# Two layers written out, norms of two groups of 280 tokens beside half tiles, and latent attention in 16 steps

## What is computed

```python
h = rmsnorm(x, g_pre_mix)
qn, qr, ckv, kr, qb, kb, vb, qc, kc, vc, alr, gc, gate = split(h @ w_in)
oa = latent_attention(qn, qr, ckv, kr)          # 8 heads, chunks of 64, meta tokens, rope
ob = windowed_attention(qb, kb, vb, sinks)      # 8 query heads, 2 key heads
loga = log_sigmoid(alr @ w_alpha + b_alpha) / 16
oc = rmsnorm(gla_scan(qc, kc, vc, loga, s0), g_gla) * silu(gc)   # 4 heads, state 128 x 256
g = sigmoid(gate)
y = g[0] * (oa @ w_up_a) + g[1] * (ob @ w_up_b) + g[2] * (oc @ w_up_c)
x = x + rmsnorm(y @ w_out, g_post_mix)
f = square(relu(rmsnorm(x, g_pre_mlp) @ w_ff1)) @ w_ff2
x = x + rmsnorm(f, g_post_mlp)
```

## Time and profile before

| | |
|---|---|
| median of 3 runs | 2607.6 us |
| the profiled execution, its own time | 2612.26 us |
| its span | 2610.5 us |
| TensorE busy | 2465.8 us |
| TensorE's mean granted clock | 0.971 |
| VectorE, ScalarE, GpSimd busy | 984.5, 943.5, 1123.3 us |
| weight splits on GpSimd | 298 of 2402 ns |

### The profile page before, as it was taken

The page is one execution under the profiler, slowest core; times in us unless marked ns, Lnnn a source line. Parts: engine busy times, 40 slices in busy tenths (PEclk is TensorE's granted clock), DMA queues, the critical chain, the costliest instruction groups (busy, mean ns, idle before and its releaser), DMA issues.

```text
span 2610.5 us, 42794 instructions
## 1 busy us (share of the span) xinstructions
PE 2465.8 (94%) x17996; PEld 2280.5 (87%) x17996; DVE 984.5 (38%) x1746; ACT 943.5 (36%) x1757; POOL 1123.3 (43%) x677
## 2 busy tenths in 40 slices
PE   7999999999999799999879999999999997999997
PEld 6999878798798799999779998878977997999996
DVE  4566435435622411111355555444256124111113
ACT  4344423332444432322334443333333544322322
POOL 5433223333355464544343432233334455645543
PEclk8999999999999899999989999999999998999998
DMA  4111311121123122222121114111211231222222
GB/s 149 56 63 55 105 54 49 45 69 56 41 73 116 42 88 89 82 89 82 64 81 57 62 56 118 41 49 47 75 49 41 81 108 49 82 89 86 85 90 84
DMA packets 57464, 189.45 MB, mean 73 GB/s; under 512 B 8048, under 2 KB 12880, under 8 KB 56624
## 3 DMA queue, kind: packets, MB, share of 16 engines
q1 hardware_dynamic: 47120, 165.90, 19.5%
q10 hardware_dynamic: 10144, 20.73, 2.5%
HBM read 172.44 MB, written 10.89 MB: 70 GB/s over the span
## 4 chain that ended last, share of the span: by engine, by line
PE 44%; DVE 3%; POOL 2%; ACT 1%; issue 1%; DVEq 0%; POOLq 0%
PE dense L695 35%; PE att L743 1%; PE att L930 1%; PE att L991 1%; DVE h_raw L1530 1%; PE att L881 1%; PE att L820 1%; POOL h_lo L1860 1%; PE att L806 0%; POOL wlo L1855 0%; DVE x L1513 0%; PE att L947 0%; PE att L964 0%; PE att L824 0%; PE att L997 0%
## 5 line engine op out<-in xcount | busy, mean ns | idle before, releaser
L1855 POOL TENSOR_TENSOR wlo<-wraw,whi 128x1024 fp32r<-128x1024 f32 x298 | 715.4, 2402 | 947.5 <-ACT whi L1060 947.5
L695 PE MATMUL dense<-h_hi,whi 128*128 128x280 f32 x3200 | 947.4, 296 | 17.5 <-ACT cproj L1098 8.3
L695 PE MATMUL dense<-h_lo,whi 128*128 128x280 f32 x3200 | 938.8, 293 | 0.0
L695 PE MATMUL dense<-h_hi,wlo 128*128 128x280 f32 x3200 | 936.6, 293 | 0.0
L695 PEld LDWEIGHTS dense<-h_hi,whi 128*128 128x128 f32 x3200 | 607.5, 190 | 41.3 <-issue 16.4
L695 PEld LDWEIGHTS dense<-h_hi,wlo 128*128 128x128 f32 x3200 | 606.4, 189 | 1.5 <-issue 0.8
L695 PEld LDWEIGHTS dense<-h_lo,whi 128*128 128x128 f32 x3200 | 607.0, 190 | 0.0
L1060 ACT ACTIVATE whi<-wraw 128x1024 fp32r<-128x1024 f32 x298 | 312.5, 1049 | 294.6 <-DMA wraw<-in_w 256.0
L695 PE MATMUL dense<-hid_lo,whi 128*128 128x280 f32 x1024 | 298.4, 291 | 0.0
L695 PE MATMUL dense<-hid_hi,whi 128*128 128x280 f32 x1024 | 297.8, 291 | 0.0
L695 PE MATMUL dense<-hid_hi,wlo 128*128 128x280 f32 x1024 | 297.6, 291 | 0.0
(11 more groups left out here) (290 smaller groups left out, 3619.5 us busy)
## 6 DMA issues: line engine op xcount, KB each, us to landing
wraw<-in_w SPq DMA_DIRECT2D x305, 512.0 KB, 3.4
x_spill<-x ACTq DMA_DIRECT2D x2, 2240.0 KB, 7.9
x<-x_spill ACTq DMA_DIRECT2D x2, 2240.0 KB, 9.2
k_cat<-k_rope ACTq DMA_DIRECT2D x16, 212.0 KB, 3.5
x<-in_x SPq DMA_DIRECT2D x4, 560.0 KB, 5.4
out_y_out<-x SPq DMA_DIRECT2D x1, 2240.0 KB, 7.3
out_c_out<-ckv ACTq DMA_DIRECT2D x2, 560.0 KB, 6.6
const<-in_const SPq DMA_DIRECT2D x1, 1112.0 KB, 10.9
```

The source lines that it names most:

```text
L695: mm = pe.matmul(bank[0:m, 0:HALF], a[:, k, o * 128:o * 128 + m], b[:, k, H[hf]], start=(k == 0 and i == 0), stop=(k == kt - 1 and i == 2))
L1855: pool.tensor_tensor(wlo[slot][:, :], wraw[slot][:, :], whi[slot][:, :].bitcast(F32), ALU.subtract).then_inc(pool_done, st.done("pool", f" ...
```

## The change

The two layers are written out in one program: the plan is one list over both layers and the work ahead of them, with its own name space for each layer (`st.layer`). The device loop, its barrier and the cleared semaphores are gone. All parameters of both layers are loaded at the start.

The five last units of `out`, the five first of `ff1`, the five last of `ff2` and the five first of a layer run as half-tiles (`("half", u, hf)`). While the second halves of the five units of `out` run, tokens 0 to 279 get the norm and are split; while the first halves of `ff1` run, tokens 280 to 559 do. The same is done from `ff2` to the next layer, where the first half of the five units of the new layer stands ahead of unit 0's second half and of `p z`. The sums of squares of the new x are made on VectorE in a buffer `nsum` and then take one matmul per half (`mean_square`), where TensorE did the sum before. `h_lo` of slices 2 and 5 is VectorE's, the other six are GpSimd's. The six PSUM banks of `SIX` serve as dense banks for `out`, `ff1`, `ff2` and the first five units of a layer, and weights have up to ten more buffers in these stretches (`slots_for`). In the prologue the same halves are used, and x comes in four quarters.

In the first head, `p z` stands behind the second half of unit 0, and four half-tiles stand between it and `p lev 0`, which also waits for the evacuations of these units. GpSimd's three memsets stand in `v arg 0`, behind VectorE's scan. The parts of head 0 behind `p vtok` (`p kv`, `p o`, `p ms`) stand one unit later than before.

The latent attention has 16 jobs; that of the first frame tile holds the 48-query tile of its pair too, and every step has its dense unit. `y` is split behind each unit of `up_b`, to `oc_hi` and `oc_lo`. The last layer has no `mean`; its x is stored by four DMAs, two for each half of the tokens.

```diff
-wraw = [at(f"wraw{s}", [P, 1024], F32, r_w[s]) for s in range(WSLOTS)]
-wlo = [at(f"wlo{s}", [P, 1024], F32R, r_w[s]) for s in range(WSLOTS)]
-whi = [at(f"whi{s}", [P, 1024], F32R, r_w[s] + 4096) for s in range(WSLOTS)]
+BASE, MLP, MIX, EDGE = range(0, 3), range(3, 5), range(5, 9), range(9, 13)
+w_at = r_w + [work + 24 * row + 8192 * i for i in range(2)] + [work + 8192 * i for i in range(4)] + [r_oc + 8192 * i for i in range(4)]
+wraw = [at(f"wraw{s}", [P, 1024], F32, w_at[s]) for s in range(len(w_at))]
...
+    def y_engine_of_lo(k):
+        return "dve" if k >= 6 else "pool"
+    def token_lo_engine(k):
+        return "dve" if k in (2, 5) else "pool"
...
+    plan = []
+    U_MIX, V_MLP = [UIDX["out", n] for n in range(KD - LAP, KD)], [UIDX["ff1", n] for n in range(LAP)]
+    U_MLP, V_NEXT = [UIDX["ff2", 32 - LAP + n] for n in range(LAP)], list(range(LAP))
+    JOBS = {"a": [("a", t, i) for t in range(4) for i in range(4)], "b": [("b", kv, i) for kv in range(2) for i in range(5)]}
+    jobs = JOBS["a"]
+    def lap(l, post, pre, first, second):
+        for hf, (at_l, units) in enumerate((first, second)):
+            for i, u in enumerate(units):
+                plan.append((at_l, ("half", u, 1 - hf)))
+                if i == 0:
+                    plan.extend([(l, ("ms", post, hf)), (l, ("norm", post, hf))])
+                if i == LAP - 2:
+                    plan.extend([(l, ("ms", pre, hf)), (l, ("tokens", pre, hf))])
...
+        order.append(("half", 0, 1))
+        gla_steps((0, "p z"), (0, "v decay"), (0, "v arg 0"))
+        for u in V_NEXT[1:]:
+            order.append(("half", u, 1))
+            if UNITS[u][0] == "cq":
+                gla_steps((0, "v arg 1"))
+            if UNITS[u][0] == "ck":
+                gla_steps((0, "v lev 0"), (0, "v arg 2"), (0, "v lev 1"), (0, "v end"), (0, "v lev 2"))
+        gla_steps((0, "p lev 0"), (0, "v kend"), (0, "v amat 0"), (0, "v amat 1"), (0, "v amat 2"))
...
+        for j in range(len(JOBS["a"]) + 2):
+            order.append(("att", "a", j))
+            dense()
...
+        for u in range(next(dn), NU):
+            kind, n = UNITS[u]
+            if u in V_MLP:
+                continue
+            plan.append((l, ("half" if u in U_MIX + U_MLP else "dense", u) + ((0,) if u in U_MIX + U_MLP else ())))
+            if kind == "up_b":
+                plan.append((l, ("split_y", n)))
+            if u == U_MIX[-1]:
+                lap(l, "post_mix", "pre_mlp", (l, U_MIX), (l, V_MLP))
+                plan.extend([(l, ("half", v, 1)) for v in V_MLP])
+        if l + 1 < DEPTH:
+            lap(l, "post_mlp", "next", (l, U_MLP), (l + 1, V_NEXT))
+            plan.append((l, ("spill",)))
+        else:
+            for i, u in enumerate(U_MLP):
+                plan.append((l, ("half", u, 1)))
+                if i == 0:
+                    plan.extend([(l, ("ms", "post_mlp", 0)), (l, ("norm", "post_mlp", 0))])
+            plan.extend([(l, ("ms", "post_mlp", 1)), (l, ("norm", "post_mlp", 1))])
+    plan += [(-1, ("square", 0)), (0, ("w", 0)), (-1, ("ms", "next", 0)), (-1, ("tokens", "next", 0)), (0, ("w", 1)),
+             (-1, ("square", 1)), (0, ("half", 0, 0)), (0, ("w", 2)), (-1, ("ms", "next", 1)), (-1, ("tokens", "next", 1)),
+             (0, ("half", 1, 0)), (-1, ("spill",)), (0, ("w", 3)), (0, ("half", 2, 0)), (0, ("w", 4)), (0, ("half", 3, 0)), (-1, ("masks",)), (0, ("half", 4, 0))]
+    for l_ in range(DEPTH):
+        layer_plan(l_)
...
+    def slots_for(l, u):
+        kind, n = UNITS[u]
+        if kind in ("out", "ff1", "ff2"):
+            if kind == "out" or (kind == "ff1" and n < 8):
+                return [*MLP, *MIX] if u in U_MIX else [*BASE, *MIX] if u in V_MLP else [*BASE] if kind == "out" else [*BASE, *MLP]
+            if kind == "ff2" and n >= 24:
+                return [*MLP, *EDGE] if u in U_MLP else [*BASE]
+            return [*BASE, *MLP]
+        return [*BASE, *EDGE] if u in V_NEXT else [*BASE]
...
+        wide = kind in ("out", "ff1", "ff2") or u in V_NEXT
+        b = min(SIX if wide else TWO, key=lambda c: bank_free[c])
...
+    def tiles_of(br, i):
+        return (0, 4) if br == "a" and i == 0 else (i,)
...
+        ys = io["y_out"].rearrange("(k p) t -> p k t", p=P)
+        for hf in range(2):
+            for g in range(2):
+                for e, k in (("dve", 4 * g + 2), ("pool", 4 * g + 3)):
+                    sp.wait_ge(by_name[e], A(e, f"x post_mlp {k} {hf}", DEPTH - 1))
+                sp.dma_start(ys[:, 4 * g:4 * g + 4, H[hf]], x[:, 4 * g:4 * g + 4, H[hf]]).then_inc(last_stored, 16)
+        sp.wait_ge(last_stored, 64)
...
-        def norm(which):
-            for hf in range(2):
-                pe.wait_ge(dve_done, A("dve", f"sum {which} 7 {hf}"))
-                mm = pe.matmul(ps[:, S0 + hf, 0:HALF], c_("ones_d"), sqsum[:, H[hf]], start=True, stop=True)
-            mm.then_inc(pe_done, st.done("pe", f"ms {which}"))
-        def mean(which):
-            for k in range(KD):
-                pe.wait_ge(act_done, A("act", f"sq {which} {k}"))
-                for hf in range(2):
-                    mm = pe.matmul(ps[:, T0 + hf, 0:HALF], c_("ones_d"), sq[:, k, H[hf]],
-                                   start=(k == 0), stop=(k == KD - 1))
-            mm.then_inc(pe_done, st.done("pe", f"ms {which}"))
+        def mean_square(which, hf):
+            part = 0 if which.startswith("post") else 1
+            pe.wait_ge(dve_done, A("dve", f"sum {which} 7 {hf}"))
+            if l < 0 and hf == 0:
+                pe.wait_ge(ones_loaded, 32)
+            mm = pe.matmul(ps[:, S0 + hf, 0:HALF], c_("ones_d"), nsum[:, part, H[hf]], start=True, stop=True)
+            mm.then_inc(pe_done, st.done("pe", f"ms {which} {hf}"))
...
+                if h == 0:
+                    for u in V_NEXT:
+                        e = evac_engine(UNITS[u][0])
+                        pe.wait_ge(by_name[e], A(e, f"evac {u} 0 1"))
...
+                    if i == 0:
+                        mm = pe.matmul(ps[0:MIXED, S0 + a, 144:144 + K_META], q_cat[:, h, META0:T], k_cat[:, h, 0:K_META],
+                                       start=False, stop=True, skip_group_check=True)
...
+        def add_square_x(which, k, hf):
+            dve.wait_ge(act_done, A("act", f"sq {which} {k} {hf}"))
+            if k >= 2:
+                dve.wait_ge(dve_done, A("dve", f"sum {which} {k - 1} {hf}"))
+            if k >= 1:
+                total = nsum[:, 1, H[hf]]
+                dve.tensor_tensor(total, total, nsum[:, 3, H[k % 2]], ALU.add).then_inc(dve_done, st.done("dve", f"sum {which} {k} {hf}"))
+        def norm(which, hf):
             src = norm_src[which]
-            dve.wait_ge(act_done, A("act", f"rstd {which}"))
+            pre = None if which == "post_mlp" and l + 1 == DEPTH else "pre_mlp" if which == "post_mix" else "next"
+            dve.wait_ge(act_done, A("act", f"rstd {which} {hf}"))
             if which == "post_mix":
-                dve.wait_ge(x_back, 16)
-                for hf in range(2):
-                    dve.wait_ge(act_done, A("act", f"evac {UIDX['out', 7]} 0 {hf}"))
+                dve.wait_ge(x_back, 16 * (l + 1))
+                dve.wait_ge(act_done, A("act", f"evac {UIDX['out', KD - 1]} 0 {hf}"))
+            else:
+                dve.wait_ge(dve_done, A("dve", f"evac {UIDX['ff2', 31]} 0 {hf}"))
             for k in range(KD):
-                t = src[:, k, :]
-                dve.scalar_tensor_tensor(t, t, p_("g_" + which, k), rstd[:, :], ALU.mult, ALU.mult
-                                         ).then_inc(dve_done, st.done("dve", f"nrm {which} {k}"))
+                t = src[:, k, H[hf]]
+                dve.scalar_tensor_tensor(t, t, p_("g_" + which, k), rstd[:, H[hf]], ALU.mult, ALU.mult
+                                         ).then_inc(dve_done, st.done("dve", f"nrm {which} {k} {hf}"))
                 if x_engine(k) == "dve":
-                    dve.wait_ge(dve_done, A("dve", f"nrm {which} {k}"))
-                    dve.tensor_tensor(x[:, k, :], x[:, k, :], t, ALU.add).then_inc(dve_done, st.done("dve", f"x {which} {k}"))
+                    dve.wait_ge(dve_done, A("dve", f"nrm {which} {k} {hf}"))
+                    dve.tensor_tensor(x[:, k, H[hf]], x[:, k, H[hf]], t, ALU.add).then_inc(dve_done, st.done("dve", f"x {which} {k} {hf}"))
+                if pre and k >= 3:
+                    add_square_x(pre, k - 2, hf)
+            if pre:
+                add_square_x(pre, KD - 2, hf)
+                add_square_x(pre, KD - 1, hf)
...
-            if s == "v decay" and h == 0:
+            if s == "v arg 0" and h == 0:
+                pool.wait_ge(dve_done, A("dve", "gla scan 0"))
...
-with nc.Fori(0, DEPTH) as l:
-    with nc.Block() as block:
-        layer(l, block)
-    for s_ in block_sems:
-        nc.sync.sem_clear(s_)
-    nc.all_engine_barrier()
...
+    program(block)
```

917 lines of the change are left out of this document (481 added, 436 removed).

## The result

| | before | after |
|---|---|---|
| median | 2607.31 us (2604.98 to 2607.72, 4 runs) | 2562.81 us (2561.44 to 2563.57, 4 runs) |
| ratio to before | | 0.9831, 95% interval 0.9814 to 0.9848 |
| span of the profiled execution | 2610.5 us | 2561.7 us |

The change saves 44.5 us of the forecast 73.7. The time lies inside the range (2490 to 2575) and outside the forecast's own (2515 to 2555), next to the rival of serial engines (2565). The parts of the sum say more than the total. The profiled executions differ by 48.8 us, of which these parts make 46.6.

The account below looks back on a forecast made before the run. TensorE, busy 2465.8 of 2610.5 us, was taken as the bound, with 215.6 us of stage losses. Savings 16.7 + 12.6 + 27 + 18.4 + 10, less 5 and 6, make 73.7: 2612.3 - 73.7 - 4.7 = 2534 us, range 2490 to 2575.

Parts of the forecast that it names:

- rival of serial engines: Half crossings: VectorE and GpSimd run one after the other, each half losing 15 us; 43 saved, 2565 us; chance 0.13.
- The steady rate: Dense matmuls in all stages: 128.3 ns each, 6.16 us per weight tile of 48, unchanged by the change.
- the attention: Latent attention in 16 steps, each with a dense tile covering TensorE's wait: saves 27 us, bounds 10 to 32.
- y: From y to out: splitting y behind each up_b tile leaves a loss of 1 us; saves 12.6, bounds 8 to 13.6.
- the tail: Behind the last tile: less work and half the tokens normed earlier leave 15.2 us; saves 16.7, bounds 12 to 20.
- the first head's wait: Before head 0's level products: a 25.0 us chain beside 12.3 us of half-tiles leaves TensorE idle 12.7 us.
- rest of the GLA heads: Next head: mean square directly ahead of its level products, with rstd between, costs 2.5 us a layer, 5 in all.
- h = 9.7: Average loss in us of one half crossing, of six; taken from (2 x 20.3 + 17.7) / 6.
- a sign of being wrong: Crossing halves losing under 5 us or over 15 would show the forecast wrong.
- 6.6: First half of a crossing: about 26 us elapsed for 19.7 us of TensorE work, so 6.6 us lost.
- 13.7: Second half of out to ff1: weight split and three linked ReLU evacuations ahead of rstd, 13.7 us lost.
- The prologue: Start to the first level products: first dense matmul some 9 us earlier, yet costs 6; bounds 14 lost to 10 gained.

Follow-up runs that it names:

- att_gap: The changed kernel with three latent-attention steps per layer (5, 9, 13) left without their dense tile, which runs behind the attention: 2580.73 us, ratio 0.9878.
- norm_first: The changed kernel with the branch norm of the second half of out to ff1 issued ahead of the first ff1 half-tile's evacuation: 2561.23 us, ratio 0.9802.
- tokens_first: The changed kernel with out to ff1's whole second-half chain (rstd, norm, rstd, splits) ahead of the ff1 half-tiles' evacuations and weight splits there: 2545.25 us, ratio 0.9728.
- lev_late: The changed kernel with one more whole tile ahead of the first head's level products in both layers: 2533.83 us, ratio 0.9691.

## Why the prediction was right in part

**Right.** The steady rate; the attention, y and the tail within 1 us each; the first head's wait (12.4 and 10.8 us, forecast 12.7) and its mechanism, a chain that the tiles beside it don't cover; the direction of every part. For the attention only half of the gain is shown to come from the mechanism that was forecast (att_gap).

**Right by luck.** The rest of the GLA heads cost 5.3 us for a forecast 5 (2.5 a layer), but layer 0 lost 8.1 and layer 1 gained 2.8. The forecast mechanism, a wait for rstd of 1.52 us ahead of the next head's level products, is there in both layers. In layer 0 a stretch at a lower granted clock followed it and in layer 1 none, 17.06 against 12.23 us for the same instructions:

```profile
138.58:155.64 17.06, 17.06 (x105) 16.99 (x105) 9.80 (x16) 1.06 (x1) 4.82 (x2) 0.70 0.08 27
1409.03:1421.26 12.23, 12.23 (x104) 12.16 (x105) 11.86 (x16) 1.06 (x1) 4.37 (x2) 1.00 0.10 35
```

In norm_first, the same program up to 840 us, that stretch of layer 0 takes 12.25 us. So 4.8 of the 5.3 come and go between executions.

**The half crossings.** The step that failed is h = 9.7. By the windows above it is 12.7 (76.3 us for six), 18 us too little. Two of the six, 17.8 and 15.5, are over the 15 that the prediction itself named as a sign of being wrong. Its terms for the norm and splits were good: VectorE's norm with its sums ran from 850.91 to 861.2, 10.3 us (10 taken), the splits from 863.40 to 871.66, 8.3 us (7). The whole first half of layer 0, from the end of the last half-tile to the end of the first that uses the half, took 26.2 us for a forecast of about 26. That it lost 7.7 and not 6.6 is a slip of counting: the prediction took off 19.7 us of TensorE's work where the six half-tiles, taken off here and in the loss before the change, are 18.5. If it did so in all six halves (its text shows it for the one), 7 of the 18 us are this slip. What was mis-sized besides stands around the norm and splits:
- In the second half of out to ff1 rstd stands twice behind linked evacuations. I counted three of 1.3 us and one split of 2.40; the first rstd came 4.2 us after its matmul and the second 6.5, since every evacuation waits for VectorE's square and this for a weight split on GpSimd. 17.8 and 15.5 were lost for 13.7. tokens_first shows that this queue, with the weight splits in it, is the cause and accounts for all that was over the forecast: 8.6 and 7.6 without it.
- In the first halves of layer 1 and of the crossing into it two weight splits stand where layer 0 has none (12.0 and 13.6 for 6.6). I took all first halves as alike and did not follow where the planner puts each split. With them moved away the halves lose 10.0 and 12.4, of which 2.1 each is the new wait for the mean square; without it they lost 7.9 and 10.3. So the splits account for 4.1 and 3.3 us. In layer 1's half that leaves next to nothing open; of the one into it some 2.6 us over layer 0's 7.7 stay open, at a granted clock of 0.92 where layer 0's half had 1.00.

**The prologue.** Forecast: gate product at 48, level products from 73 to 78. Measured: 52.2, and 78.3 to 87.9. The gate product is four us late, with TensorE waiting 5.17 for the split of the fourth tile's weight; one more us comes from the chain, and 4.5 from the level products at half speed, which I had counted for the second layer's head only as a lump of 3.4. The rows of TensorE at these places:

```profile
14.63 0.55 PE L780 MATMUL dense<-h_hi,whi 128*112 128x280 f32 x1 [3.37 <-POOL h_lo L2000]
...
40.67 0.46 PE L780 MATMUL att<-h_hi,whi 128*128 128x280 f32 x1 [5.17 <-POOL wlo L1995]
...
52.22 0.50 PE L806 MATMUL att<-kra,const 16*128 16x280 f32 x1 [0.54 <-DVE kra L1545]
...
78.34 0.34 PE L826 MATMUL att<-level 128*64 128x64 f32 x1 [12.39 <-DVE cproj L1554]
```

The first dense matmul came 7.8 us sooner than before, and nothing of it was left at the gate product: with 144 dense matmuls ahead of it (18.5 us) 33.7 us were lost up to there, where the kernel before, with 48, lost 27.6.

**The rival of serial engines** gave 2565 and looks right by its time, but not by its mechanism: it had h = 15 from the sum of all work in every half, where the runs show a first half that loses 7.7 and a second half that falls to 8.6 by order alone, with the same work. Its time was met because the halves lost 12.7 and the prologue 10 more than forecast.

**The missed opportunity.** lev_late saves more (29.7 us) than all the crossings: the change left about two tiles' worth of wait ahead of each layer's first level products (12.4 and 10.8 us), and such a wait was paid twice, once idle and once at half speed on the work behind it.

## What to carry to other kernels

Where one half's norm is to run beside the other half's matmuls, follow each engine's queue, not only the chain: put the whole chain of the half ahead of the evacuations that the cover itself makes, and hold them in spare banks. See where a planner's background work (here weight splits) falls in each copy of a crossing, since copies that look alike lose up to 6 us more or less, 3 to 4 of them from the splits. Look also at what the moved work then stands ahead of: it took 2.1 us back here. Put one more tile ahead of a consumer whose chain is a few us too long: the wait goes, and so does the half-speed stretch behind it.

## What the runs showed of the hardware that was not expected

The granted clock differs between executions of the same instructions. From 120 to 400 us the changed kernel and norm_first run the same program (their edit comes at 840 us), and the second did 52 matmuls more in that time at 0.99 instead of 0.96:

```profile
120.00:400.00 280.00, 270.10 (x1882) 245.66 (x1881) 144.41 (x265) 107.70 (x170) 90.70 (x70) 0.96 0.22 66
```

```profile
120.00:400.00 280.00, 270.13 (x1934) 244.62 (x1933) 150.36 (x275) 112.98 (x182) 93.33 (x71) 0.99 0.23 68
```

When its edit comes, norm_first is 7.5 us ahead. That is as much as several of the edits are worth: norm_first's profiled execution took 2555.75 us and its median is 2561.23. The Trainium skill (TensorE: Matmul & The Clock Gate, Part 1: The HAM clock gate, What's actually happening) calls the ramp at a kernel's start "run-variable"; these rows show such a difference in mid-kernel, of which that passage doesn't speak. An edit of this size has to be read from its own stage.
